# Opening of a two-layer decoder step: x in four pieces, first two column groups tile by tile, parameter rows turned in portions

## The reference, cut to what matters

```python
xn = rms_norm(x, g[0])                 # x * rsqrt(mean(x*x)) * g
proj = xn @ w_in                       # (2048, 4096); xb is the first half
xb, yb = proj[..., :D_RNN], proj[..., D_RNN:]
xc, new_buf = causal_dwconv(xb, buf0, conv_w, conv_b)
```

## Time and profile before

| | us |
|---|---|
| median of 3 runs | 2566.1 (2565.02 to 2566.55) |
| the profiled execution, its own time | 2564.02 |
| its span in the trace | 2562.3 |
| PE busy | 2458.0 (96%) |
| DVE busy | 1600.3 (62%) |
| ACT busy | 1107.4 (43%) |
| POOL busy | 230.8 (9%) |

### The profile page before, as it was taken

The page is one execution under the profiler, slowest core; times in us unless marked ns, Lnnn a source line. Parts: engine busy times, 40 slices in busy tenths (PEclk is TensorE's granted clock), DMA queues, the critical chain, the costliest instruction groups (busy, mean ns, idle before and its releaser), DMA issues.

```text
span 2562.3 us, 53902 instructions
## 1 busy us (share of the span) xinstructions
PE 2458.0 (96%) x20255; PEld 2387.2 (93%) x20255; DVE 1600.3 (62%) x2710; ACT 1107.4 (43%) x1567; POOL 230.8 (9%) x352
## 2 busy tenths in 40 slices
PE   6999999999999999999788999999999999999998
PEld 5999989999999999999786767989999999999997
DVE  4888577664566556665864446476664666456655
ACT  4378444443344334444542334353443444334434
POOL 1010121000000000002132300220000000000011
PEclk9999999999999999999999999999999999999999
DMA  6554644655565556555444622545555565555552
GB/s 219 165 173 146 199 154 135 190 180 183 170 194 177 185 170 191 180 181 172 117 129 133 214 68 75 181 132 165 185 181 182 174 188 175 186 173 189 180 182 78
DMA packets 428659, 425.80 MB, mean 166 GB/s; under 512 B 29116, under 2 KB 416276, under 8 KB 428264
## 3 DMA queue, kind: packets, MB, share of 16 engines
q1 hardware_dynamic: 422872, 413.53, 51.5%
q0 software_dynamic: 5248, 8.16, 1.0%
q10 hardware_dynamic: 432, 2.66, 0.3%
HBM read 420.86 MB, written 3.95 MB: 166 GB/s over the span
## 4 chain that ended last, share of the span: by engine, by line
PE 85%; DVE 9%; ACT 3%; issue 2%; SPq 0%; DMA 0%; ACTq 0%; DVEq 0%; POOL 0%
PE acc L1803 26%; PE acc L1804 25%; PE acc L1805 25%; DVE lo L1171 3%; PE acc L2112 1%; DVE x L1447 1%; ACT hi L792 1%; PE mis L2130 1%; PE mis L2208 1%; PE mis L2159 1%; PE mis L2207 1%; DVE lo_ahead L1171 1%; SPq L557 0%; DVE f L1442 0%; DVE lo_ahead L1179 0%
## 5 line engine op out<-in xcount | busy, mean ns | idle before, releaser
L1171 DVE TENSOR_TENSOR lo<-raw,hi 128x1024 fp32r<-128x1024 f32 x724 | 876.7, 1228 | 769.7 <-ACT hi L792 768.7
L792 ACT ACTIVATE hi<-raw 128x1024 fp32r<-128x1024 f32 x724 | 756.8, 1058 | 816.0 <-PE acc L1805 809.4
L1803 PE MATMUL acc<-xnh,hi 128*128 128x264 f32 x3568 | 1021.6, 286 | 23.7 <-DVE lo L1171 14.3
L1805 PE MATMUL acc<-xnh,lo 128*128 128x264 f32 x3568 | 1016.9, 285 | 0.0
L1804 PE MATMUL acc<-xnl,hi 128*128 128x264 f32 x3568 | 1015.7, 285 | 0.0
L1803 PEld LDWEIGHTS acc<-xnh,hi 128*128 128x128 f32 x3568 | 677.2, 190 | 26.0 <-issue 15.6
L1804 PEld LDWEIGHTS acc<-xnl,hi 128*128 128x128 f32 x3568 | 678.0, 190 | 0.5
L1805 PEld LDWEIGHTS acc<-xnh,lo 128*128 128x128 f32 x3568 | 675.7, 189 | 0.0
L1803 PE MATMUL acc<-hh,hi 128*128 128x264 f32 x2048 | 581.4, 284 | 0.0
L1805 PE MATMUL acc<-hh,lo 128*128 128x264 f32 x2048 | 580.7, 284 | 0.0
L1804 PE MATMUL acc<-hl,hi 128*128 128x264 f32 x2048 | 580.0, 283 | 0.0
(11 more groups left out here) (341 smaller groups left out, 2134.3 us busy)
## 6 DMA issues: line engine op xcount, KB each, us to landing
raw<-in_w_ffn_g SPq DMA_DIRECT2D x192, 512.0 KB, 4.5
raw<-in_w_ffn_u SPq DMA_DIRECT2D x192, 512.0 KB, 4.0
raw<-in_w_ffn_d SPq DMA_DIRECT2D x192, 512.0 KB, 4.2
raw<-in_w_rg_in SPq DMA_DIRECT2D x64, 512.0 KB, 5.3
raw<-in_w_rg_o SPq DMA_DIRECT2D x32, 512.0 KB, 4.6
raw<-in_w_mla_o SPq DMA_DIRECT2D x32, 512.0 KB, 3.4
cpage_h<-in_cache_kv_latent SPq DMA_DIRECT2D x48, 256.0 KB, 4.8
raw<-in_w_dkv SPq DMA_DIRECT2D x8, 512.0 KB, 3.7
```

Of the source, the lines that this page charges most:

```text
L792: act.activation(high_at(c, e)[:, :, 0:n], raw[:, c % RAW, :, 0:n], ACT.Copy).then_inc(s.hi_ready, 1)
L1171: dve.tensor_tensor(low_at(c, e)[:, :, 0:n], raw[:, c % RAW, :, 0:n], high_at(c, e)[:, :, 0:n].bitcast(F32), ALU.subtract).then_inc(s.lo_r ...
L1803: pe.matmul(out, wh, xh, start=start, stop=False)
L1805: return pe.matmul(out, wl, xh, start=False, stop=stop)
```

## The change

- ACT issues the identity alone, then x in four DMAs of 512 columns each, the sample rows behind the first, and the rest of the constants last.
- SP issues the four pieces of the norm rows, then the weight chunks 0 to 7 in order of use (q by q, alternating between the two groups) without a wait for x, then 14 of the 28 late pieces of the parameter rows (1,280 rows), then chunk 8 and on. POOL issues the other 14 (1,280 rows) after the first piece of x. Its two state copies to the output move behind the gate weights, and those behind the first two convolutions.
- PE turns the norm rows first, then tiles 0 to 3 of x, and runs groups 0 and 1 with `first_pair`, turning tile j+4 behind tile j. Group 2 follows, with the turning of parameter portions 1 and 2 behind its first chunk and `row_sum` behind its third; group 3, with portions 3, 4 and 5 behind its first three chunks; then groups 4 and 5.
- ACT copies each portion into `PT`: 1 and 2 between its high parts of chunks 9 and 10, and 3, 4 and 5 behind those of chunks 13, 14 and 15. A warming Sqrt comes at the start.
- DVE takes the tiles in, makes low parts of x and of chunks 0 to 7 in between, then low parts of chunks 8 and 9, the sum of squares, those of 10 and 11, `rx`, then copies out both groups, convolves both, and does the 17 parameter steps; low parts of chunks 12 to 15 come behind that.

```diff
+FIRST_HI = {7: 4, 8: 5, 11: 6, 12: 7}
...
-        ptrows = sb("ptrows", [P, PT_TILES, P], F32, xn_at)
+        ptrows = sb("ptrows", [P, PT_TILES, P], F32, h_at + KT * T * 4)
...
+        PT_ORDER = (5, 0, 1, 2, 3, 4)
+        norm_pieces = [piece for piece in row_pieces if piece[1] >= NORM_TILE]
+        late_pieces = row_pieces[len(norm_pieces):]
+        TURN_BANKS = (mis[2], mis[3], acc[0], acc[1])
...
@@ SP
-            for n, (q, t, src) in enumerate(row_pieces):
-                if n % 4:
-                    sp.dma_start(ptrows[q:q + src.shape[0], t, :], src).then_inc(s.rows_in[0], 16)
-            sp.wait_ge(s.x_in, 32)
-            for a in range(2):
-                for q in range(4):
-                    chunk(C_RGX + 4 * a + q, rows4(I["w_rg_in"][0], q, 256 * a))
+            for q, t, src in norm_pieces:
+                sp.dma_start(ptrows[q:q + src.shape[0], t, :], src).then_inc(s.norm_in, 16)
+            for q in range(4):
+                for a in range(2):
+                    chunk(C_RGX + 2 * q + a, rows4(I["w_rg_in"][0], q, 256 * a))
+            for q, t, src in late_pieces[0::2]:
+                sp.dma_start(ptrows[q:q + src.shape[0], t, :], src).then_inc(s.rows_in[0], 16)
@@ POOL
+            pool.wait_ge(s.x_in[0], 32)
+            for q, t, src in late_pieces[1::2]:
                 pool.dma_start(ptrows[q:q + src.shape[0], t, :], src).then_inc(s.rows_in[1], 16)
...
-            pool.wait_ge(s.pt_ready, 6)
+            pool.wait_ge(s.pt_ready, 3)
+            for n in range(2):
+                conv_columns(n)
+                conv_tail(n, (gs, cv)[n])
             for n in range(2):
                 gate_weights(0, n)
@@ ACT
+            params(0)
+            act.wait_ge(s.pt_ready, 1)
+            for j in range(KT):
+                if j < 4:
+                    split(C_RGX + j)
+                act.wait_ge(s.x_tile, j + 1)
+                act.activation(xnh[:, j, :], x[:, j, :], ACT.Copy, scale=PT[:, PT_NORM + j:PT_NORM + j + 1])\
+                    .then_inc(s.xn_hi, 1)
+                last = act.activation(sq_h[:, j, :], x[:, j, :], ACT.Square)
+                if j in FIRST_HI:
+                    split(C_RGX + FIRST_HI[j])
+            last.then_inc(s.sq_done, 1)
+            for c in range(8, 10):
+                split(C_RGX + c)
+            for n in range(1, 3):
+                params(n)
+            for c in range(10, 12):
+                split(C_RGX + c)
             root(N_X0, D)
...
-            for c in range(8, 12):
+            for c in range(12, 20):
                 split(C_RGX + c)
+                if 13 <= c < 16:
+                    params(c - 10)
@@ DVE
+            turn_in(0)
+            turn_in(1)
             for j in range(KT):
+                if j < 4:
+                    split(C_RGX + j)
+                if j + 2 < KT:
+                    turn_in(j + 2)
+                low(xnl, xnh, PT_NORM, j, XN_0)
+                if j in FIRST_HI:
+                    split(C_RGX + FIRST_HI[j])
+            split(C_RGX + 8)
+            split(C_RGX + 9)
+            dve.wait_ge(s.sq_done, N_X0 + 1)
+            row_sums(sq_h[:, :, :])
+            split(C_RGX + 10)
+            split(C_RGX + 11)
             inverse(N_X0, rx)
+            def first_conv_pairs():
+                dve.wait_ge(s.chunk_used, C_RGX + 8)
+                for buf, banks in ((gs, mis[0:2]), (cv, acc[2:4])):
+                    for m in range(2):
+                        evac(dve.tensor_tensor(buf[:, m, :], banks[m][:, 0:T], rx[:, :], ALU.mult))
+                for a, buf in enumerate((gs, cv)):
+                    dve.wait_ge(s.cw_ready, a + 1)
+                    dve.wait_ge(s.acc_read, 2 * a + 2)
+                    conv_pair(buf, lambda m, u, v, a=a: f[:, 2 * a + m, u:v], 4, cwr, 14 * a)
+                    dve.wait_ge(s.tail_saved, a + 1)
-            conv_pairs(0, leads=(1,))
+            first_conv_pairs()
@@ PE
+            pe.wait_ge(s.ident_in, 16)
+            pe.wait_ge(s.norm_in, 16 * len(norm_pieces))
+            turn_params(0)
+            for j in range(4):
+                turn_x(j)
+            first_pair(C_RGX, 0, XN_0, ahead=False, after=lambda j: turn_x(j + 4) if j + 4 < KT else None)
             pe.wait_ge(s.ones_set, 2)
+            pe.wait_ge(s.x_tile, KT)
+            group(C_RGX + 8, 4, 2, xnh, xnl, xn(XN_0), after=lambda q: (turn_params(1), turn_params(2)) if q == 0 else
+                  row_sum(N_X0) if q == 2 else None, free=0)
+            group(C_RGX + 12, 4, 3, xnh, xnl, xn(XN_0), after=lambda q: turn_params(q + 3) if q < 3 else None)
             for a in range(2):
-                group(4 * a, 4, a, xnh, xnl, xn(XN_0), between=(lambda: row_sum(N_X0)) if a else None)
-            with pe.Fori(1, 3) as i:
-                for a in range(2):
-                    group(4 * a, 4, a, xnh, xnl, xn(XN_0), g_off=i * 2, c_off=i * 8)
+                group(C_RGX + 16 + 4 * a, 4, 4 + a, xnh, xnl, xn(XN_0))
```

More of the change, by code:

```diff
@@ L300, in build @@
         s.rows_in = [sem(f"rows_in{n}") for n in range(2)]
-        s.x_in = sem("x_in")
+        s.x_in = [sem(f"x_in{n}") for n in range(4)]
+        s.norm_in = sem("norm_in")
+        s.ident_in = sem("ident_in")
         s.ones_set = sem("ones_set")
@@ L823, in root @@
                     .then_inc(s.rms_ready, 1)
[L825 to L839, removed]
             def block_end(b, n_f, acc_done, split_c):
@@ L870, in block_ramp @@
                 split_c(11)
[L872 to L882, removed]
+            def params(n):
+                act.wait_ge(s.turned, 1 + (KT + n if n else 0))
+                k = PT_ORDER[n]
+                w = min(512, PT_END - 512 * k)
+                bank = TURN_BANKS[0 if n % 2 == 0 else 1]
+                act.activation(PT[:, 512 * k:512 * k + w], bank[:, 0:w], ACT.Copy).then_inc(s.pt_ready, 1)
+            act.dma_start(kc[:, K_ID:K_ID + P], I["consts"][:, K_ID:K_ID + P]).then_inc(s.ident_in, 16)
@@ new lines, in _ @@
+            for n in range(4):
+                src = I["x_prompt"][0][:, 512 * n:512 * n + 512].rearrange("(t p) d -> p t d", p=P)
+                act.dma_start(xrows[:, :, 512 * n:512 * n + 512], src).then_inc(s.x_in[n], 16)
+                if n == 0:
+                    act.dma_start(xsrows[:, :], I["x_sample"][:, 0, :]).then_inc(s.x_in[0], 16)
+            act.dma_start(kc[:, P:], I["consts"][:, P:]).then_inc(s.const_in, 16)
+            act.wait_ge(s.ones_set, 2)
+            act.activation(warm[:, :], eps[:, :], ACT.Sqrt)
@@ L887, in _ @@
             act.activation(soft[:, 1, :], soft[:, 0, :], ACT.Exp, scale=-1.0).then_inc(s.par_step, 1)
-            for c in range(8, 12):
+            for c in range(12, 20):
                 split(C_RGX + c)
-            with act.Fori(1, 3) as i:
-                for c in range(8):
-                    split(C_RGX + 4 + c, off=i * 8)
+                if 13 <= c < 16:
+                    params(c - 10)
+            for c in range(20, 28):
+                split(C_RGX + c)
             def gate_tanhs(i, b):
@@ L1264, in _, with turn_in @@
             dve.memset(ones[:, :], 1.0).then_inc(s.ones_set, 1)
-            for j in range(KT):
[L1266 to L1285, removed]
-            inverse(N_X0, rx)
+            def turn_in(j):
+                dve.wait_ge(s.turned, j + 2)
+                dve.tensor_copy(x[:, j, :], TURN_BANKS[(j + 1) % 4][:, 0:T]).then_inc(s.x_tile, 1)
+            dve.wait_ge(s.pt_ready, 1)
+            turn_in(0)
+            turn_in(1)
+            for j in range(KT):
+                if j < 4:
[11 more added lines that the diff above has]
+            split(C_RGX + 11)
+            inverse(N_X0, rx)
+            def first_conv_pairs():
[8 more added lines that the diff above has]
+                    dve.wait_ge(s.tail_saved, a + 1)
             def conv_pairs(i, leads=(0, 1), between=None):
@@ L1805, in mm3, with group @@
                 return pe.matmul(out, wl, xh, start=False, stop=stop)
-            def group(c, n, g, xh, xl, ready, g_off=0, c_off=0, tiles=2, between=None, banks=None, free=None):
+            def group(c, n, g, xh, xl, ready, g_off=0, c_off=0, tiles=2, between=None, banks=None, free=None, after=None):
                 banks = banks or acc[2 * (g % 2):2 * (g % 2) + 2]
@@ L1829, in group, with first_pair @@
                     last.then_inc(s.chunk_used, 1)
-            def first_pair(c, g, xbase):
+                    if after:
+                        after(q)
+            def first_pair(c, g, xbase, ahead=True, after=None):
                 banks = (mis[0:2], acc[2 * ((g + 1) % 2):2 * ((g + 1) % 2) + 2])
@@ L1842, in first_pair @@
                             e = 2 * q + a
+                            wh, wl = high_at(c + e, e if ahead else None), low_at(c + e, e if ahead else None)
                             for m in range(2):
                                 cols = slice(m * P, m * P + P)
```

(27 more changed lines are left out.)

20 lines of the change are left out of this document (12 added, 8 removed).

## The result

The changed kernel took 2573.6 us (median of 8 runs, 2570.46 to 2576.53), the kernel before 2564.84 (8 runs, 2563.11 to 2566.55): ratio 1.0029, interval 1.002 to 1.0038. It is slower by 8.8 us or 0.3%, and the interval lies wholly above 1. The profiled execution took 2570.46, its span is 2568.8, 6.5 more than that of before.

What follows compares the result with a forecast made beforehand. PE's matmuls bound the kernel, with DVE equally the bound up to group 3. 22.1 us more, less a head start of 20.1, plus 1.0 for the clock gave about 2.9 us longer: 2569.0 us, range 2562 to 2575.

Steps and rivals of the forecast that it cites:

- What bounds the kernel: Whole kernel: a train of PE matmuls; in the opening up to group 3, DVE as much the bound as PE.
- The new wait: PE before chunk 12: idles 15.2 us, as DVE needs 18.3 us from `row_sum` to that chunk's low part.
- A second wait: PE before chunk 16: waits 2.3 us for DVE, then runs that chunk slowly at 4.75.
- Cold restart of chunk 12: PE at chunk 12, behind the long wait: 5.3 us for the chunk, 2.4 of it for the cold clock.
- Loads: Opening loads: both queues at 0.39 MB a us, terms adding to 15.1 us, so chunk 3 lands at 17.8.
- Clock in the tile stage: PE among the first tiles: idle waits may let the clock relapse, 1.85 us each where PE binds; 1.0 taken.
- The slower rival: PE from 11 to 45 us: clock stays low, a tile takes 3.6 us, not 1.98; chance 0.26.
- The sum: Opening up to the gates: 22.1 us more, less a 20.1 head start, plus 1.0 clock; gates at 119.0 against 116.05.
- my own case: Opening: DVE as the bound, head start spent in its wait; 2563 to 2571 us, chance 0.63.
- the clock case: Tile stage: three relapses or more move everything behind `row_sum` by 4.6, with late chunk 3 by 6.8; 2574 to 2576.
- the signs: Opening: first real matmul near 12, `row_sum` at 53 to 59, gates at 115 to 122, waits about 15 and 2.3.
- The kept head start: PE before chunk 12: low part does not hold PE, 2547 us; beyond 0.2% if wait under 7.2; chance 0.11.

Runs made afterwards that it cites:

- before_par_later: Kernel before, with DVE's 17 parameter steps moved one pair of groups later; 2568.03 us in one run, beside 2567.75 for the kernel before.
- par_later: Changed kernel with DVE's 17 parameter steps moved between the work for groups 3 and 4; 2564.43 us against 2567.75 for the kernel before, ratio 0.9998.
- turned_late: Changed kernel with parameter portions 3 to 5 turned in group 5 instead of group 3; 2570.18 us in one run, beside 2565.81 for the kernel before.
- kept_warm: Changed kernel with 110 extra, unused matmuls on PE in the wait before chunk 12; 2567.98 us in one run, beside 2565.81 for the kernel before.
- loads_late: Changed kernel, POOL's rows held until chunk 3 landed, remaining constants issued behind the last tile; 2565.76 us in one run, beside 2567.75 for the kernel before.
- dve_order: turned_late plus DVE's pieces reordered from chunk 8's low part on, low parts before convolutions; 2562.26 us in one run, beside 2565.81 for the kernel before.
- all_parts: Edits of loads_late, turned_late and dve_order (list slightly changed), `row_sum` behind group 2's first chunk; 2552.54 us against 2565.81 for the kernel before, ratio 0.9948.

## Why the prediction was right or wrong

**What bounds the kernel: right.** PE's 96% told nothing of this change; that DVE and PE arrived together at group 3 did, and before_par_later and par_later show it from both sides.

**The new wait: right.** 18.3 us from `row_sum` to the restart were summed, 18.6 put into the dates (74.1 - 55.5; the 0.3 has no term), and 18.0 measured; a wait of 15.2 forecast and 14.5 measured. A second wait of 2.3 was forecast and 2.9 measured, and its cause, high parts that stand behind turned portions, is shown by turned_late. From the restart to the gates 43.9 were forecast and 43.8 measured. Cold restart of chunk 12: 2.4 taken, 2.7 by kept_warm, 1.5 to 2.5 by the time that chunk 12 took in four runs.

**Loads: the term that was mis-sized.** "Chunk 3 lands at 17.8 (chunk 1 at about 13)": ACT had chunk 1 at 17.56 and chunk 3 by 21.5. The sharing by packets was right, 111 to 117 in the same microsecond as in the earlier trace rows:

```profile
q10 hardware_dynamic: 111, 0.21, 62.8%
q1 hardware_dynamic: 117, 0.11, 34.9%
```

but the sum rate was 0.32 MB a us, not the 0.39 that both queues had reached with x in large packets. It was 0.32 on average from 3 to 20 us too: 5.5 MB, as much as x, four chunks, the constants, the norm rows and POOL's rows. The sum had these at 15.1 us, 0.36 a us; at 0.32 they take 17, so 2 us more. Nor was chunk 3 the one that ACT waited for: it waited for chunk 2 until 19.84, and came to chunk 3 1.7 later, at 21.53. So DVE began the low part of chunk 3 at 23.03 and not at 18.9, 4.1 late: 2.0 until chunk 2 was there, 1.7 for ACT's work on it, and 0.4 in which DVE was still at the tile before. (The way from 18.9 to tile 3 at 21.5 was taken too long: 20.5 and the low part of x, 0.42, give 20.9. The other 0.6 has no term.)

Chunk 1 came 4.5 late, and tile 3 on PE at 26.9, not 21.5: 5.4 of the 5.6 by which `row_sum` came later than forecast (61.1 against 55.5). loads_late takes 2.3 of them back.

**Clock in the tile stage: 1.0 taken, about 1.7 there.** From tile 3 on PE ran without a relapse, but up to 23.5 it ran at the lower level (last section), and from 19.93 on it did so without waiting for anything:

```profile
22.17 0.59 PE L1836 MATMUL mis<-xnh,hi 128*128 128x264 f32 x1
...
23.65 0.29 PE L1836 MATMUL acc<-xnh,hi 128*128 128x264 f32 x1
...
24.85 0.39 PE L1836 MATMUL mis<-xnh,hi 128*128 128x264 f32 x1
...
25.68 0.29 PE L1836 MATMUL acc<-xnh,hi 128*128 128x264 f32 x1
...
26.88 0.39 PE L1836 MATMUL mis<-xnh,hi 128*128 128x264 f32 x1
```

Six matmuls of `acc` and the turning of a tile took 22.17 - 19.93 = 2.24 at the lower level and 24.85 - 23.65 = 1.20 at the higher; six of `mis` took 1.48 and 0.83. That is 1.7 us, and as an estimate from these rows tile 3 could have started at 25.2. DVE would have had its low part ready at about 25.1. So of the 5.4 about 3.7 are the loads' and 1.7 the clock's. loads_late shows the same from the other side: there chunk 1 came 3.2 earlier, but PE stayed at the lower level through tile 1, and tile 3 started at 24.52, 2.4 earlier. The slower rival, a clock that stays low among the tiles, thus came in a small measure, 0.7 more than I had taken and not 4.6; the larger part of the delay is the one that stood beside it in that case ("with 20 for chunk 3's landing").

**The sum.** Forecast for the gates: 119.0, measured 122.9. By terms: 5.6 more for `row_sum`; the 1.0 of the clock, which stood apart from it, is in that already and comes off; 0.6 less for DVE's queue (18.0, not 18.6); 0.1 less behind the restart. Forecast for the time 2.9 us more, measured 6.9 at the gates, 7.1 at the end sum and 8.8 in the medians. The last step is the scatter of the rest (2202.3 and 2202.9 in the two profiled executions); whether the medians hold anything more of the change than its 7.1 is open.

The wait's place, cause and length were forecast; the size of the loss was not, for it came out at three times the 2.9. The range, 2562 to 2575, held 2573.6, but my own case reached from 2563 to 2571 and did not: what held it is the upper end, which had been set for the clock case, and that is luck in part. I gave 0.64 to "within 0.2%" and 0.25 to slower; the case that came was the second. The terms that took it there are the load term and, for 0.7, the clock. Three of the signs were missed by the same delay: the first real matmul came at 14.5 and not near 12, `row_sum` at 61.1 and not at 53 to 59, the gates at 122.9 and not by 122. The waits, their places and the unchanged time behind the gates came as said.

**The kept head start: did not come, as forecast.** Its condition, a wait under 7.2 us, was not met; dve_order and all_parts show that it can be, by another order on DVE.

## What to carry to other kernels

An engine that starts earlier gains only what the next engine's queue lets through: here PE began 24.1 us earlier and the gates came 6.9 later. Before moving work forward, find the one instruction behind which the next stage's operands stand (here the low part of chunk 12), and sum what stands before it in its engine's program order; the small dependent steps and the convolutions that no one waits for yet belong behind it. A load that opens the kernel shares the DMA engines with the loads issued near it, so hold back those that are needed later; here that gave 2.3 us at `row_sum`.

## What the runs showed of the hardware that I had not expected

In the first stretch the granted clock of the profile does not fit the pace of the matmuls. In the changed kernel these two windows have the same clock of 1.00 (columns as in the earlier trace rows):

```profile
22.00:23.00 1.00, 1.00 (x6) 1.00 1.10 348
25.00:26.00 1.00, 1.00 (x9) 1.00 1.15 317
```

and these are the starts of matmuls in them:

```profile
22.56 0.42 PE L1837 MATMUL mis<-xnl,hi 128*128 128x264 f32 x1
22.78 0.42 PE L1838 MATMUL mis<-xnh,lo 128*128 128x264 f32 x1
...
25.20 0.28 PE L1838 MATMUL mis<-xnh,lo 128*128 128x264 f32 x1
25.32 0.28 PE L1836 MATMUL mis<-xnh,hi 128*128 128x264 f32 x1
```

A pitch of 0.22 us is that of the stretch at 0.50 (1.2 GHz), 0.12 that at 1.00 (2.4 GHz). The change between them falls at 23.5. So by their pace the opening ran at the lower level until then, and so did the parameter transposes of the kernel before, 4.94/22 = 0.22 us each, where the eight of group 2 in the changed kernel took 1.04 (from 54.04), 0.13 each. A turned portion thus cost about 0.5, where I had priced it at 0.85: the 0.44 of the earlier trace rows is the joined busy time of two transposes that overlap, and half of it is not the time of one.

A wait did not always lower the clock. Behind PE's wait of 2.60 before chunk 8 of the kernel before, the granted clock was 0.64 in 68 to 69 and 0.50 in 69 to 70; behind the 2.56 of par_later it was 0.51 in 92 to 94; behind the 2.18 of dve_order it stayed at 1.00.

The rest of the kernel, the same instructions in the same order, varied by 8.7 us between profiled executions (2201.2 to 2209.9), as much as the 8.8 by which the medians differ.
